# Query and key slots of a mixer projection: sixteen column slots turned into wide slots, their halves added on VectorE

## What is computed

```python
def hybrid_mixer(u, positions, w_in, ...):
    proj = u @ w_in
    xa, ya, q, k, v, g, sb, sc, sh, gates = jnp.split(proj, cuts, axis=-1)
    xa = causal_depthwise_conv(xa, lru_conv_w) + lru_conv_b
    ha = rg_lru(xa, lru_w_a, lru_b_a, lru_w_x, lru_b_x, lru_lambda)
    ...
    ret = retention(q.reshape(...), k.reshape(...), v.reshape(...), positions)

def rope(t, positions):
    ...
    t1, t2 = t[..., :half], t[..., half:]
    return jnp.concatenate([t1 * cos - t2 * sin, t1 * sin + t2 * cos], axis=-1)
```

## Time and profile before

| | |
|---|---|
| median of 3 runs | 1984.29 us (1983.97 to 1985.08) |
| the profiled execution | 1985.03 us |
| its span | 1983.2 us, granted clock 0.998 |
| TensorE, matmuls | 1968.8 us busy, 99%, 10554 |
| TensorE, weight loads | 1697.3 us busy, 86%, 10554 |
| VectorE | 1333.0 us busy, 67%, 1644 |
| ScalarE | 996.0 us busy, 50%, 1393 |
| GpSimd | 110.0 us busy, 6%, 211 |
| DMA | mean 186 GB/s |

### The profile page before, as it was taken

The page is one execution under the profiler, slowest core; times in us unless marked ns, Lnnn a source line. Parts: engine busy times, 40 slices in busy tenths (PEclk is TensorE's granted clock), DMA queues, the critical chain, the costliest instruction groups (busy, mean ns, idle before and its releaser), DMA issues.

```text
span 1983.2 us, 25950 instructions
## 1 busy us (share of the span) xinstructions
PE 1968.8 (99%) x10554; PEld 1697.3 (86%) x10554; DVE 1333.0 (67%) x1644; ACT 996.0 (50%) x1393; POOL 110.0 (6%) x211
## 2 busy tenths in 40 slices
PE   9999999999999999999999999999999999999998
PEld 7888998888888888888889888888888888978886
DVE  6756778557676674766669765576666666777665
ACT  5445465354444544544544654444454445754444
POOL 1002000000000000100310000000010101110001
PEclk9999999999999999999999999999999999999999
DMA  8565456535665556565654555456655664445552
GB/s 282 184 224 190 141 181 209 191 128 170 212 212 191 172 190 214 169 206 190 222 178 155 170 205 170 153 188 211 214 170 175 234 230 152 137 156 181 189 193 105
DMA packets 241141, 369.18 MB, mean 186 GB/s; under 512 B 6775, under 2 KB 171927, under 8 KB 241022
## 3 DMA queue, kind: packets, MB, share of 16 engines
q1 hardware_dynamic: 236000, 352.34, 53.3%
q0 software_dynamic: 4528, 14.85, 2.3%
q10 hardware_dynamic: 494, 0.32, 0.1%
HBM read 366.28 MB, written 1.08 MB: 185 GB/s over the span
## 4 chain that ended last, share of the span: by engine, by line
PE 98%; ACT 1%; DVE 1%; issue 0%; POOL 0%; DMA 0%; DVEq 0%; POOLq 0%; ACTq 0%
PE ps L1790 23%; PE ps L1810 22%; PE ps L2060 20%; PE ps L1792 12%; PE ps L1900 6%; PE ps L1780 2%; PE ps L1781 2%; PE ps L1779 2%; PE ps L1859 2%; PE ps L2027 1%; PE ps L1879 1%; PE ps L1999 1%; PE ps L1835 1%; PE ps L2229 1%; PE ps L2187 0%; PE ps L2206 0%
## 5 line engine op out<-in xcount | busy, mean ns | idle before, releaser
L1173 DVE TENSOR_TENSOR w_lo<-raw,w_hi 128x1024 fp32r<-128x1024 f32 x638 | 751.8, 1221 | 316.5 <-ACT w_hi L728 313.8
L728 ACT ACTIVATE w_hi<-raw 128x1024 fp32r<-128x1024 f32 x638 | 639.8, 1053 | 297.4 <-PE ps L1810 174.7
L1790 PE MATMUL ps<-u,w_hi 128*128 128x512 f32 x1968 | 470.2, 391 | 0.0
L1790 PEld LDWEIGHTS ps<-u,w_hi 128*128 128x128 f32 x1968 | 362.5, 188 | 71.6 <-issue 0.8
L1792 PEld LDWEIGHTS ps<-u,w_lo 128*128 128x128 f32 x1968 | 252.3, 191 | 9.6
L1792 PE MATMUL ps<-u,w_lo 128*128 128x256 f32 x1968 | 255.3, 283 | 0.0
L2060 PE MATMUL ps<-w_hi,u 128*128 128x512 f32 x640 | 201.6, 390 | 0.0
L2060 PEld LDWEIGHTS ps<-w_hi,u 128*128 128x128 f32 x640 | 120.2, 188 | 24.8
L1810 PE MATMUL ps<-w_hi,h_hi 128*128 128x512 f32 x448 | 138.4, 390 | 0.0
L1810 PE MATMUL ps<-w_lo,h_hi 128*128 128x512 f32 x448 | 138.1, 389 | 0.0
L1810 PE MATMUL ps<-w_hi,h_lo 128*128 128x512 f32 x448 | 138.0, 389 | 0.0
(11 more groups left out here) (316 smaller groups left out, 2553.8 us busy)
## 6 DMA issues: line engine op xcount, KB each, us to landing
raw<-in_w_mix_in_dram SPq DMA_DIRECT2D x112, 1024.0 KB, 5.1
raw<-in_ffn_w_in_dram SPq DMA_DIRECT2D x80, 1024.0 KB, 5.2
raw<-in_ffn_w_out_dram SPq DMA_DIRECT2D x44, 1024.0 KB, 5.0
raw<-in_w_ret_out_dram SPq DMA_DIRECT2D x16, 1024.0 KB, 5.1
raw<-in_w_up_dram SPq DMA_DIRECT2D x16, 1024.0 KB, 5.5
raw<-in_w_down_dram SPq DMA_DIRECT2D x16, 1024.0 KB, 4.9
raw<-in_w_in_dram SPq DMA_DIRECT2D x9, 1024.0 KB, 5.4
raw<-in_w_lru_out_dram SPq DMA_DIRECT2D x8, 1024.0 KB, 5.1
```

Source lines behind the costliest of these rows:

```text
L728: A(parts(n)[0][:, part], raw[i % RAW][:, part], ACT.Copy).then_inc(heads_done, 1)
L1173: V.tensor_tensor(parts(n)[1][:, part], raw[i % RAW][:, part], parts(n)[0][:, part], ALU.subtract)\
L1790: M(ps[:, bank0 + a, :], hi[:, k, P * a:P * a + P], u[:, :, k, :], start=k == 0, stop=False)
```

## The change

The q and k slots become wide. In `WIDE` their names are put in front. What else follows from that in the code that isn't in the diff: TensorE runs `wide_slot` for them; q_j waits for the eviction of xa slot 2j + 1 for j = 0 and 1, and for `col_summed` two slots back for j = 2 and 3; k0 and k1 wait for the sums of q2 and q3, and ya0 and ya1 for those of k2 and k3. ScalarE now waits for each q and k slot to end and copies its second half into one area, `k_sum` (the second half of `act2`; the first half is in use by the LRU gates). That one area serves all eight slots, so the copy of slot j waits until the rotation of slot j - 1 is done. VectorE adds the first half to it in place, waits for the add, and rotates from it.

```diff
-WIDE = ("ya", "sc", "sh", "sb")
+WIDE = ("q", "k", "ya", "sc", "sh", "sb")
...
+        k_sum = act2[:, 1, :].rearrange("p (a n) -> p a n", a=2)
...
-                        if name in ("xa", "ya", "sc", "sh", "sb") or name in ("ga", "g", "gb", "gc") and j % 2 == 1:
+                        if name in ("xa", "q", "k", "ya", "sc", "sh", "sb") or name in ("ga", "g", "gb", "gc") and j % 2 == 1:
                             emptied(n)
...
+                        elif name in ("q", "k"):
+                            if name == "k" and j == 0:
+                                act.wait_ge(q_ready.sem, q_ready.at(l, 4))
+                            elif j >= 1:
+                                rotated = q_ready if name == "q" else k_ready
+                                act.wait_ge(rotated.sem, rotated.at(l, j))
+                            A(k_sum, col_halves(j)[1], ACT.Copy).then_inc(col_low.sem, 1)
...
-            def rope(l, j, bank, dst, sig):
-
-                pv = ps[:, bank, :].rearrange("p (a n) -> p a n", a=2)
+            def rope(j, pv, dst, sig):
+
...
-                        if name == "q":
-                            if j == 0:
-                                dve.wait_ge(sines, 2)
-                            dve.wait_ge(slot_used, n + 1)
-                            rope(l, j, bank, q_t, q_ready)
-                        elif name == "k":
-                            dve.wait_ge(slot_used, n + 1)
-                            rope(l, j, bank, k_t, k_ready)
                         if name in WIDE:
                             i = col_index(name, j)
-                            part = tiles({"ya": a2, "sc": a1}[name])[:, pair, :] if name in ("ya", "sc") else col_sum(j)
+                            if name in ("q", "k"):
+                                part = k_sum
+                            else:
+                                part = tiles({"ya": a2, "sc": a1}[name])[:, pair, :] if name in ("ya", "sc") else col_sum(j)
                             dve.wait_ge(col_low.sem, col_low.at(l, i + 1))
                             V.tensor_tensor(part, col_halves(j)[0], part, ALU.add).then_inc(col_summed.sem, 1)
+                            if name in ("q", "k"):
+                                if name == "q" and j == 0:
+                                    dve.wait_ge(sines, 2)
+                                dve.wait_ge(col_summed.sem, col_summed.at(l, i + 1))
+                                rope(j, part, *((q_t, q_ready) if name == "q" else (k_t, k_ready)))
```

## The result

The changed kernel takes 1988.34 us (median of 22 runs, 1986.04 to 1990.34), the kernel before 1984.61 us beside it (22 runs, 1983.83 to 1985.66). The ratio is 1.0019, 95% interval 1.0013 to 1.0025: 3.7 us slower, just inside the 0.2% that I had called no change. The forecast was 1986.2 us. The sign, the place and the one new stall were right; 2.1 us were missing. Two executions, one of `wait_only` and one of the kernel before beside it, ran far longer (3292 and 7355 us) at a mean granted clock of 0.56 and 0.26, and no number in this text uses them.

What follows compares the result with a forecast made beforehand. TensorE's back-to-back matmuls (busy 99%) bound the kernel. Per layer, stall 2.45 less 0.12 less 1.38 gives +0.95 us, +1.9 in all: 1986.2 us against the median of 1984.29; 8-in-10 range 1983.8 to 1989.2.

Steps and rivals of the forecast that it cites:

- the one new stall: TensorE at q2, each layer: waits for VectorE's add of q0's halves behind the convolution; 2.45 us, bounds 2.2 to 2.9.
- TensorE's gain: Wide q and k slots: 0.19 us less for q0, 0.17 for each of seven gated slots, 1.38 us a layer.
- the gap rule of the Trainium skill: TensorE matmuls at N/2.4 + 2.5 ns each: saving only 0.04 us a slot, kernel ending some 1.6 us later.
- the row of before: TensorE's column form in the old profile: 0.36 us for three matmuls of 256 columns, cited against the gap rule.
- the handover: From a VectorE result to TensorE's next matmul: 0.14 us, putting q2's start at 239.10.
- The slot behind the wait: q2 starts on an idle TensorE with no gate to drain: 5.65 us rather than 5.77, giving 0.12 back.
- The other engines: VectorE's cycle grows from 4.96 to 5.6 to 5.7 us, SBUF products cost nothing, ScalarE's copies fit its gaps.
- a slack of 0.15: TensorE at q3: q1's sum handed over at 245.28, q3 wanted at 245.43, so no second stall.
- The rival of the single sum area: q and k slots: ScalarE's copy not hidden, VectorE's cycle 6.6 us against 6.45; total +4.9, 1989.2 us; chance 0.07.
- The clock: Behind each q2 stall, half a slot at 1.2 GHz: 2.8 us a layer, total +7.5, 1991.8 us; chance 0.08.
- other rivals: Sum area 0.07 (1989.2 us); stall doesn't come 0.08 (1981.5); wide form saves nothing 0.04 (1988.2).
- the forecast alone: Stall 2.2 to 2.9, saving 0.14 to 0.19 a slot: 1984.6 to 1988.2 us with scatter; chance 0.70.

Runs made afterwards that it cites:

- wait_only: The kernel before plus one wait: TensorE holds q2 until VectorE has made the first product of q0's rotation; 1988.68 us, ratio 1.0020.
- the kernel without stalls: The changed kernel with ScalarE's and VectorE's work reordered for wide q and k slots, q copies put in unused k_t; 1982.01 us, ratio 0.9987.
- warm8: The changed kernel with 8 spare 128x128 fp32 matmuls into idle PSUM bank 7 ahead of q2, inside the stall; 1986.56 us, ratio 1.0008.
- early_add: The changed kernel with VectorE's add of q0's halves moved ahead of the convolution of xa3; 1989.12 us, ratio 1.0023.
- the run with k alone: Half of the change against the kernel before: k slots wide, q kept in column form; 1983.37 us, ratio 0.9993.
- wait_long: The kernel before plus a longer wait: TensorE holds q2 until the whole rotation of q0 is done; 1992.95 us, ratio 1.0041.
- q_only: Half of the change against the kernel before: q slots wide, k kept in column form; 1990.46 us, ratio 1.0030.

## Why the prediction was right or wrong

**TensorE's gain: right.** 0.17 a gated slot and 0.18 for q0 (0.19 forecast) were measured in the changed kernel (229.51 - 223.85 = 5.66 against 5.84 before). As a time of its own the gain shows in the kernel without stalls: -2.6 us of the 2.8 expected. By the gap rule of the Trainium skill (page "TensorE: Matmul & The Clock Gate", section "Back-to-back issue gap") it would have been 0.6, an estimate of 0.04 for each of sixteen slots; the runs speak against it, as the row of before did.

**The stall: right in cause and place, and nearly in number.** One wait a layer, at q2, released by the add behind the convolution. q2 was to start at 239.10 and started at 238.97, 2.35 us late where I had 2.45. The term that was off is the handover: I took 0.14 from a row at the start of the kernel, and behind q0's add it took 0.05 (0.06 in layer two, in `wait_only`, `warm8` and `early_add`). The slot behind the wait took 5.69 in layer two for 5.65. Net of the gains +0.9 a layer for +0.95; the executions without a fall of the clock lie 1.5 us above the kernel before, for +1.9. That their median meets the forecast to 0.1 us is in part luck: the kernel before itself measured 0.3 higher beside them (1984.61) than in the three runs that I started from.

**The other engines: right.** VectorE's cycle is 5.69 for 5.6 to 5.7, the first SBUF product 0.69 for 0.69, the copies lie in ScalarE's gaps. q3 had a slack of 0.15 by the sum and 0.20 in layer two (sum of q1 at 1066.59, handover 0.05, q3 at 1066.84). The rival of the single sum area is refuted by the trace (no wait at q3 or later) and by the run with k alone.

**The clock: the step that failed.** The sum put this term at nothing. I had it among the rivals with 0.08 and priced it at 2.8 us a layer. It came in 19 of 22 executions, and one fall costs 1.6 us in the trace and 1.1 to 2.1 by the distance between groups of runs (2.1 and 1.2 in the changed kernel, 3.35 for two falls). Both the chance and the size were off, in opposite directions: with the right size and one fall in most executions the forecast would have been 1988. What misled me was the weighing, not a missing row. The trace of before held a wait of 1.1 us at full clock and a clock that fell when TensorE had nothing to do; my 2.45 lay in between, and I took the lower end as the rule. The section of the Trainium skill that I quoted there (page "TensorE: Matmul & The Clock Gate", section "A second HAM failure mode: psum-queue depth-cycling") describes frequent short idle times in a cycle through PSUM banks and a clock that goes back and forth between the two levels. The trace agrees on the levels and on the kind of wait, with 0.50 behind the wait for a bank pair, but here a single idle time of 2.0 us was enough.

**The range** of 1983.8 to 1989.2 held the median only because it was stretched for other rivals; the forecast alone ended at 1988.2. (Its lower end is mis-added: a stall of 2.2 less 0.12 less eight times 0.19 is +0.6 a layer, not +0.4. Nothing hangs on it.) "No change" by the bound of 0.2% holds at 0.19%, with an interval that reaches over it.

Open: why the distances between groups of runs go from 1.1 to 2.1 us. The five falls in the traces all last 3.4 us at 0.50, so none can cost more than 1.7, half of that. Four of them begin 0.9 to 1.4 us behind the first matmul of the held slot, and those cost 1.57 to 1.60; the fifth, in `wait_long`, begins 0.4 us ahead of it. What the rest of the distance is no run shows. The wait for the first load, at the very start, goes from 2.1 to 2.6 us over the ten traces and is one source of scatter. Open too is why the clock falls behind one stall and not behind its twin.

## What to carry to other kernels

Doubling the PSUM that a step holds halves the number of steps until its banks are wanted again: q0's are wanted by q2 here and were wanted by k0, two slots later, before. Before counting the gain, look for the moment at which that engine is furthest behind, because one late eviction can eat the gain of many steps; what was saved ahead of the wait is lost in it.

A stall of TensorE costs its own length and then, in a share of the executions, a stretch at half clock behind it. Runs of one kernel that fall in groups 1 to 2 us apart, sorted by their mean clock, were the mark of it here; filling the idle time with a few spare matmuls that surely end in time is a quick test.

Where an engine is behind, sort its queue by who waits: sums and weights that TensorE wants first, results that are used much later last.

## What the runs showed of the hardware

In the traces the granted clock fell behind 3 of 4 idle times of 2.0 us (one of two in the changed kernel, both in `q_only`), 1 of 2 of 2.3 us, 1 of 2 of 3.1 us, and neither of 2 of 1.6 us. By their times at least one fall came in 19 of 22 executions with two idle times of 2.0 us, in three of four with 3.1 us and in none of nine with 1.6 us. For equal stalls it fell in one layer and not in the other of the same execution.

A clock of 1.00 during the idle stretch itself says nothing: in four of the five falls it went down only 0.9 to 1.4 us after TensorE had begun to work again. Each time it stood at 0.50 for 3.4 us, whichever stall came before.

The handover from a VectorE result to the matmul that waited for it took 0.05 to 0.06 us where it waited for a sum or a product of a q slot (one row at the start of the kernel, from which the forecast took it, has 0.14).

An fp32 matmul of 128x128 by 128 columns is two records and takes 0.218 us, so 8 fill 1.75 us.
